# A hybrid encoder layer on one core: experts with the fewest picks in blocks of 128 slots, the last norm inside the expert stage, and four smaller edits

## The reference

```python
mixed = g[:, :, 0] * (ya @ w_pa) + g[:, :, 1] * (yb @ w_pb) + g[:, :, 2] * (yc @ w_pc)
x = _layer_norm(DN_ALPHA * x + mixed @ w_out, ln1_g, ln1_b)

f = _moe(x, router_w, router_b, exp_w1, exp_b1, exp_w2, exp_b2)
ple = jax.nn.sigmoid(x @ ple_gate_w + ple_gate_b) * (p @ ple_w)
x = _layer_norm(DN_ALPHA * x + f + ple, ln2_g, ln2_b)
```

```python
gu = jnp.einsum('nmd,ndf->nmf', xs.reshape(NB, M, D), w1[block_e]) + b1[block_e][:, None]
g_ = jnp.minimum(gu[..., :D_FF], SWIGLU_LIMIT)
up = jnp.clip(gu[..., D_FF:], -SWIGLU_LIMIT, SWIGLU_LIMIT)
act = (up + 1.0) * g_ * jax.nn.sigmoid(SWIGLU_ALPHA * g_)
y = jnp.einsum('nmf,nfd->nmd', act, w2[block_e]) + b2[block_e][:, None]
```

## The kernel before

| stage | us from the span's start |
|---|---|
| `stage_sb_sample` (attention of the sample rows over the cache) | 700 to 789 |
| `stage_mlstm` | 789 to 882 |
| `stage_mix` (not touched) | 882 to 1388 |
| `stage_out` (projection w_out, first norm, rows turned into x1T) | 1388 to 1517 |
| `stage_route` (router, picks, slot tables, the ple term into residual rows) | 1517 to 1697 |
| `stage_experts` | 1698 to 2630 |
| `stage_combine` (second norm) | 2630 to 2677.6 |

## Time and profile before

### The profile page before, as it was taken

How to read it: one execution, slowest core, us unless ns; L and a number is a source line. 1 busy time by engine, 2 the same in 40 slices (tenths; PEclk the granted TensorE clock), 3 DMA queues, 4 the chain that set the end, 5 groups by cost and what they waited for, 6 DMA issues and landing times. The chain is left out here.

```text
span 2677.6 us, 40379 instructions
## 1 busy us (share of the span) xinstructions
PE 2475.0 (92%) x14989; PEld 2220.9 (83%) x14989; DVE 1596.6 (60%) x2522; ACT 1312.1 (49%) x2091; POOL 660.6 (25%) x491
## 2 busy tenths in 40 slices
PE   7999999998888899999989889799999999999990
PEld 6988797896657899999987567788898989989980
DVE  3666421207648555445534466688888888887774
ACT  4666320116435534334322223477777777776662
POOL 1000100004201011010113205144444544444433
PEclk8999999999989999999999999899999999999995
DMA  8321232203486565565534312699998989988854
GB/s 249 87 66 42 83 114 89 83 16 126 141 282 159 133 162 137 123 161 142 138 97 156 135 59 73 214 291 284 294 291 279 290 265 297 281 270 275 272 167 169
DMA packets 389435, 468.10 MB, mean 175 GB/s; under 512 B 17470, under 2 KB 312602, under 8 KB 389311
## 3 DMA queue, kind: packets, MB, share of 16 engines
q1 hardware_dynamic: 367213, 395.82, 47.5%
q0 software_dynamic: 17760, 60.34, 8.9%
q10 hardware_dynamic: 4338, 10.23, 1.0%
HBM read 397.63 MB, written 68.71 MB: 174 GB/s over the span
## 5 line engine op out<-in xcount | busy, mean ns | idle before, releaser
L3426 PE MATMUL banks<-slot_rowsT,expert_w_high 128*128 128x288 f32 (+2 forms) x2048 | 556.5, 353 | 4.9 <-DVE expert_w_low L3563 4.2
L3429 PE MATMUL banks<-slot_rowsT,expert_w_low 128*128 128x144 f32 (+2 forms) x2048 | 491.7, 240 | 0.0
L3429 PEld LDWEIGHTS banks<-slot_rowsT,expert_w_low 128*128 128x128 f32 x2048 | 396.1, 193 | 1.4
L3426 PEld LDWEIGHTS banks<-slot_rowsT,expert_w_high 128*128 128x128 f32 x2048 | 390.7, 191 | 7.0 <-DVE expert_w_low L3563 4.4
L3480 ACT CAST expert_w_high<-xT_then_expert_w 128x2048 fp32r<-128x2048 f32 x127 | 235.7, 1904 | 2.0 <-DMA xT_then_expert_w<-in_exp_w 2.0
L3563 DVE TENSOR_TENSOR expert_w_low<-xT_then_expert_w,expert_w_high 128x2048 fp32r<-128x2048 f32 x95 | 214.4, 2284 | 16.0 <-ACT expert_w_high L3480 16.0
L3348 POOL TENSOR_TENSOR expert_w_low<-xT_then_expert_w,expert_w_high 128x2048 fp32r<-128x2048 f32 x32 | 146.7, 4584 | 208.8 <-ACT expert_w_high L3480 208.8
L2214 PE MATMUL banks<-xT_chunk_high,w_gates_high 128*128 128x384 f32 x576 | 193.1, 335 | 4.5 <-DVE xT_chunk_low L2286 4.5
L2215 PE MATMUL banks<-xT_chunk_low,w_gates_high 128*128 128x384 f32 x576 | 193.0, 335 | 0.0
L2216 PE MATMUL banks<-xT_chunk_high,w_gates_low 128*128 128x384 f32 x576 | 192.9, 335 | 0.0
L3604 DVE TENSOR_TENSOR expert_w_low<-expert_w,expert_w_high 128x1024 fp32r<-128x1024 f32 x128 | 159.1, 1243 | 52.0 <-ACT expert_w_high L3508 52.0
(11 more groups left out here) (541 smaller groups left out, 6192.3 us busy)
## 6 DMA issues: line engine op xcount, KB each, us to landing
xT_then_expert_w<-in_exp_w SPq DMA_DIRECT2D x126, 1024.0 KB, 7.9
expert_w<-in_exp_w SPq DMA_DIRECT2D x32, 2048.0 KB, 9.6
w_gates<-in_w_in SPq DMA_DIRECT2D x72, 512.0 KB, 4.4
cached_k<-in_cache_sb_k SPq DMA_DIRECT2D x16, 1024.0 KB, 10.4
cached_v<-in_cache_sb_v SPq DMA_DIRECT2D x16, 1024.0 KB, 11.5
w_stream<-in_w_in SPq DMA_DIRECT2D x48, 256.0 KB, 4.5
w_proj<-in_w_pa SPq DMA_DIRECT2D x24, 512.0 KB, 5.2
w_stream<-in_w_in SPq DMA_DIRECT2D x16, 512.0 KB, 5.1
```

Source lines behind the costliest of these rows:

```text
L3426: nc.tensor.matmul(out[:, 0:2 * SLOTS].rearrange("p (a s) -> p a s", a=2)[:, :, 0:width], hi, xgT[:, par, k, :, 0:width], start=(place == ...
L3429: last = nc.tensor.matmul(out[:, 0:width], lo, xgT[:, par, k, 0, 0:width], start=False, stop=(place == DT - 1), skip_group_check=True)
```

## The change

Six edits come together. (1) In `stage_sb_sample`, GpSimd, ScalarE and VectorE also prepare three fp32r parts of `m.w`, a selector for them and fp32r copies of the masks; `scores` in `stage_mlstm` uses these with one fp32r pass for each call. (2) In `divide`, two linked operations become one. (3) In `stage_out`, pieces 3 to 12 of w_out are loaded by three transfers at the stage's start, some of them into a buffer of the routing stage, and pieces 13 to 15 by one. (4) Two of the three chunks of logits are multiplied at the end of `stage_out` ahead of turn 8; in `stage_route` the turns of p are spread over the first units. (5) The four experts with the fewest picks get blocks of 128 slots, the next eight 144, the next twelve 160; for a width of 128 the products of the last 64 slots are not made. (6) `stage_combine` is gone; its work is a class whose parts run at the end of each engine's program in `stage_experts`, the scale and shift are loaded during the last block, and SP's loads of the residual rows follow GpSimd's last wait.

```diff
-FEW = ((12, 144), (12, 160))
+FEW = ((4, 128), (8, 144), (12, 160))
 # stage_sb_sample, GpSimd: two memsets and three affine_selects; then ScalarE and VectorE:
+                if s == 7:
+                    act.wait_ge(parts_zeroed, 2)
+                    nc.scalar.copy(m.w_parts[0:H], m.w[:]).then_inc(parts_high, 1)
+                if s == 9:
+                    act.wait_ge(parts_left, 1)
+                    nc.scalar.copy(m.w_parts[32:32 + H], m.w[:])
+                if s == 11:
+                    nc.scalar.copy(rest[:], m.w[:]).then_inc(parts_high, 1)
+                if s == 13:
+                    for n, tile in enumerate((g.ident, g.causal, g.causal_s)):
+                        nc.scalar.copy(m.masks[:, n, :], tile[:])
+                if s == 8:
+                    dve.wait_ge(parts_high, 1)
+                    nc.vector.tensor_tensor(m.w[:], m.w[:], m.w_parts[0:H].bitcast(F32), ALU.subtract
+                                            ).then_inc(parts_left, 1)
+                if s == 12:
+                    dve.wait_ge(parts_high, 2)
+                    dve.wait_ge(parts_left, 1)
+                    nc.vector.tensor_tensor(m.w_parts[64:64 + H], m.w[:], rest[:].bitcast(F32), ALU.subtract)
 # stage_mlstm
-                nc.tensor.matmul(g.bank[0][:], g.ident[:], mask[:].unsqueeze(1).broadcast_to([P, H, P]), start=True,
+                nc.tensor.matmul(g.bank[0][:], m.masks[:, 0, :],
+                                 m.masks[:, 2 if i == NT - 1 else 1, :].unsqueeze(1).broadcast_to([P, H, P]), start=True,
-                    last = nc.tensor.matmul(g.bank[0][:, h * P:(h + 1) * P], g.sel[:, h, :], m.w[:, cols],
+                    last = nc.tensor.matmul(g.bank[0][:, h * P:(h + 1) * P], m.sel_parts[:, h, :], m.w_parts[:, cols],
-                link(nc.vector.tensor_scalar(den[:, 0], num[:, :, HD], -1.0, None, ALU.mult))
-                link(nc.vector.tensor_tensor(den[:, 1], den[:, 0], num[:, :, HD], ALU.max))
+                link(nc.vector.scalar_tensor_tensor(out=den[:, 1], in0=num[:, :, HD], scalar=-1.0, in1=num[:, :, HD],
+                                                    op0=ALU.mult, op1=ALU.max))
 # stage_out
+        RUNS = ((WR, 2), (WR + 2, DT - WR - 2), (DT, PIECES - DT + WR), (WR + PIECES, len(pieces) - WR - PIECES))
-            for n in range(WR, len(pieces)):
-
-                sp.wait_ge(w_split, n - WR + 1)
-                early.load(sp, n)
+            for (first, count), landed in zip(RUNS, run_in):
+                half, k = pieces[first]
+                if first + count == len(pieces):
+                    sp.wait_ge(w_split, WR)
+                sp.dma_start(raw_pieces(first, count), early.source[:, k:k + count, half * 512:(half + 1) * 512]
+                             ).then_inc(landed, 16)
+                    sp.wait_ge(w_split, WR + PIECES)
+                    route.load_ahead(sp)
+                if i == NT + 1:
+                    pe.wait_ge(route.rw_in, 32)
+                    pe.wait_ge(moved, 12)
+                    pe.wait_ge(sum_ready, 2 * NT - 2)
+                    for c in range(2):
+                        router_logits(nc, g, route.rw, x1T, c)
                 if i >= 2:
                     turn(i - 2)
 # stage_route, TensorE (turn_p: the turns of p; ScalarE and VectorE take the parts in the same order)
+            router_logits(nc, g, rw, x1T, 2).then_inc(logit_sum, 1)
+            turn_p(0)
+            turn_p(1)
+                if n == 0:
+                    turn_p(2)
+                if n in (3, 4):
+                    turn_p(n)
+                    pe.wait_ge(p_moved, 3)
                     turn_gates()
 # stage_route, SP: p tiles 3 to 6 go ahead of the second half's weight pieces
 # stage_experts, TensorE
                     for bank, r, half in OUTS:
+                        if r and width <= S0:
+
+                            if f == FT - 1:
+                                pe.nop().then_inc(y_ready, 1)
+                            continue
 # stage_experts, SP in the last block, then after it
+                if not ahead:
+                    sp.wait_ge(w2_split, 4 * n + 4)
+                    last_norm.load_norm(sp)
             each_block(sp, step)
+            last_norm.sync(sp)
+    def sync(self, sp):
+        sp.wait_ge(self.all_out, 1)
+        for i in range(NT):
+            sp.dma_start(self.res[:, i, :], self.g.residual_d[i * P:(i + 1) * P, :]).then_inc(self.res_in[i], 16)
```

309 lines of the change are left out of this document (181 added, 128 removed).

## The result

The changed kernel takes 2654.66 us (median of 3 runs, 2653.9 to 2657.2) against 2684.75 before: a ratio of 0.9902, 95% interval 0.9873 to 0.9931. The forecast was 2653, range 2635 to 2672. The profiled execution after has a span of 2652.2 us against 2677.6: 25.4 less.

| stretch | before | after | difference | forecast |
|---|---|---|---|---|
| start to sample attention's first product (not touched) | 700.23 | 697.84 | -2.4 | 0 |
| sample attention, to mLSTM's first product | 89.46 | 88.48 | -1.0 | +1 |
| mLSTM, to the merge's first product | 95.28 | 90.89 | -4.4 | -4.5 |
| merge (not touched) | 506.77 | 507.39 | +0.6 | 0 |
| output projection, first to last product | 114.72 | 105.67 | -9.1 | -7 |

What follows compares the result with a forecast made beforehand. No single bound: TensorE full in places, VectorE nearly full in mLSTM, GpSimd's w1 round in the experts. Terms sum to -28.5, giving 2650.8 from the profiled execution or 2656.3 from the median; forecast the middle, 2653, range 2635 to 2672.

Steps and rivals of the forecast that it cites:

- mLSTM: mLSTM scores: cheaper products leave VectorE binding at 5.37 us; nine tiles give 3.1, before the first tile 1.4; -4.5.
- Sample attention: Sample attention: added ScalarE copies and VectorE subtractions mostly fall into ScalarE's waits for TensorE; +1, between 0 and +7.
- Output projection: Start of the output projection: w_out pieces issued at once let tile 0 end earlier; -7, bounds -8 and -4.
- Logits: Router logits: two chunks fill TensorE's wait, 6.4 us earlier, and p turns move behind later units; -6, bounds -9.5 and -3.
- Narrow blocks: Four expert blocks of 128 slots: 5 us of TensorE work become idle time, gain 0; block 0 alone saves 1.3.
- The border, +0.3: Experts: one more split of the loop over blocks costs 1.56 us, mostly taken by TensorE's new slack; +0.3.
- the round of the earlier trace: Experts: GpSimd's w1 subtraction with ScalarE's and VectorE's work on 192 slots sets the block's period, 27.19 us, whatever its width.
- Last norm: Last norm: residual loads directly follow the last scatter without the drain, VectorE starts 11.3 earlier; -11, bounds -12.5 and -7.5.
- A: Narrow expert blocks: TensorE is the bound there, giving 20 us more, total 2634; chance 0.10.
- B: Narrow expert blocks: TensorE's clock falls; mild form 2665, chance 0.05; full form 2718, chance 0.03.
- C: Experts: the fourth-lowest expert has 129 picks or more, adding two blocks, +54, total 2707; chance 0.02.
- D: Several stages: gains are handed back through copies on the path, a delayed last turn, a returning drain; 2662 to 2674; chance 0.12.

Runs made afterwards that it cites:

- third_loop: Changed kernel with three TensorE loops of widths (4, 144), (8, 144), (12, 160), so no blocks of 128 slots: 2661.96 us, ratio 0.9928.
- before_gather_first: Kernel before, with only GpSimd's gather put ahead of its wait for the last scatter: 2671.83 us, ratio 0.9965.
- gather_first: Changed kernel with GpSimd's gather for the block after next issued ahead of the wait for the last scatter: 2641.32 us, ratio 0.9843.
- late_adds_on_vector: Changed kernel with the norm's shift of the last two tiles added by VectorE instead of GpSimd: 2653.94 us, ratio 0.9901.
- few_back: Changed kernel with the block widths of before, (12, 144) and (12, 160), so no blocks of 128 slots: 2654.82 us, ratio 0.9907.

## Why the prediction came out

**Right in total**: 1.7 us from the median, with the sign, the size, and most of the places of the gains; that it came so close is in part luck, as the last paragraph adds up. Point by point:

- *mLSTM*: in the loop mechanism and size are right, VectorE's pitch of 5.37 and TensorE's waits included: from VectorE's first product to the ninth tile's it is 47.52 us before and 44.05 after, 3.5 less for the 3.1 of the sum. The 1.4 in front of the first tile did not come: TensorE waits there for `ml_v`, and its next product starts 0.3 us later than before. That the stage still gives 4.4 is luck: 1.2 us fewer lie behind the ninth tile's product.
- *Sample attention*: the added copies cost nothing that shows, and the sign of the term is wrong. The stretch is 89.12 to 89.46 us in three profiles of kernels with the old code and 88.46 to 88.48 in ten of the eleven with the new (90.10 in third_loop): 0.9 less. Why is open.
- *Output projection*: mechanism right, mis-sized by 2 us: 9.1 for 7. Tile 0 after took 13.46 us, more than the 12.8 of the prediction (1.4 for the low clock of the first seven products, 0.63 us and more for six of them, and a wait of 0.83 for a split). What the prediction read wrongly is the kernel before: TensorE "is full only from about 1412", but tile 0 ended at 1414.07.
- *Logits*: right, 6.8 for 6.4, and the delay of the last turn is 5.93 for 5.9. Of the most that the term could give, 9.5, the prediction took 3.5 off, mainly for VectorE's units; only 0.8 were missing.
- *Narrow blocks*: right in the step that decided (27.14 and idle time in place of products), wrong in the two small terms. "Narrower products save up to 1.35/0.72" in block 0, -1.3, did not come: block 0 takes 40.66 us after and 39.65 before. TensorE waits there for w1 (6.65 us at 1692.83 after, 4.19 before, ending in both 18.5 us behind the first turn), so a shorter product only lengthens the wait. The border, +0.3, was +1.0.
- *The experts as a whole*: the step that failed is that "the round of the earlier trace rows" was the only one in a block. There is a second on GpSimd, scatter, landing, gather, landing, and TensorE's turns, with a few tenths of a microsecond to spare, and when it slips behind VectorE's subtraction the next block is 1.7 to 5.2 us longer at once (17 of 18 times). One profile of the kernel before showed hardly any of it: its few long periods were read as borders (the earlier trace rows at 28.75), while before_gather_first has 27.61 at the same place. By the kernels with the early gather, of the 6.6 us 2.7 lie between the widths (1.0 the border, 1.5 block 0, whose cause is open), 0.3 are the other edits (911.7 against 911.4), and about 3.5 the gathers of these two executions.
- *Last norm*: mechanism right up to VectorE's start; the first row took 3.29 us for the 3.3 that the prediction gave without a row for it. The size is the lower bound that the prediction named, -7.5 "if the same drain comes back": -7.1.

**The rivals.** A fell (27.14, not 23). B's fall of the clock was seen and cost nothing: 0.94 and 0.87 lie above the 0.80 where the prediction put the crossing; the rule of the Trainium skill ("TensorE: Matmul & The Clock Gate", section "HAM oscillation — how this bites in real kernels") describes what happens behind the gap of 3.5 us that blocks 1 to 3 have in gather_first. The trace agrees: ahead of the gap that ends at 1734.82 the clock is 1.00 (1722 to 1730), behind it 0.69 (1734 to 1738). The idle time absorbs it. C did not occur (2048 pairs of products of the first layer are 32 blocks of 64). Of D, one part in three was true, the drain.

The total was helped by luck, errors of both signs: 3.9 us too much for the norm and 7.6 too much for the experts met 6.8 too little from sample attention to the logits and 1.8 on stages that were not touched. Open is why gathers are late oftener with the changed code than before: in two profiles of before they cost 6.2 and 10.0 us of the way, in the changed kernel 9.7, in late_adds_on_vector 13.1 and in few_back 15.8 (each against the kernel with the early gather and the same widths).

## What to carry to other kernels

Ask of a steady loop not only which round sets its period but how much slack the second round has, and on what it would run aground: a queue that waits for a landing ahead of an unrelated load turns half a microsecond of jitter into four. Work that is left out pays only on the engine that closes the round, and only until the next limit; here 4 us of products were worth nothing, and 1.3 us of exits were worth 1.3 in one block and 0.4 to 0.6 in the two behind it. A drain that is moved is not gone until other work covers it.

The experiments lead to a version that beats both kernels: the gather ahead of the wait, the last two additions on VectorE, no exits for slots that the narrow blocks do not have, and pieces issued early, 2630.18 us, 0.980 of before (0.976 to 0.984).

## What I had not expected of the hardware

An indirect transfer that GpSimd issues 0.22 us after VectorE has begun a 128x2048 subtraction took 2.96 us to issue, and 1.00 us when it began 0.12 us before; all 18 slow issues ended 3.17 to 3.18 us behind the subtraction's start. GpSimd's drain in the program with indirect transfers took 6.6 to 6.7 us whether it followed a wait (before), nine additions (after) or seven (late_adds_on_vector), beside 0.11 behind nine additions in a program without them. TensorE's mean clock fell to 0.94 and 0.87 in blocks where it idled 3.4 to 5 us, with no effect on the block's time.
